# Inverse roots of the norms in a two-model transformer kernel: ScalarE square root and VectorE reciprocal in place of ScalarE logarithm and exponential

## The reference, cut to what matters

```python
def rms_norm(x, g):
    xf = x.astype(jnp.float32)
    y = xf * lax.rsqrt(jnp.mean(xf * xf, axis=-1, keepdims=True) + EPS)
    return (y * g.astype(jnp.float32)).astype(x.dtype)

def layer_norm_2(x, g, b):
    x32 = x.astype(jnp.float32)
    mu = jnp.mean(x32, axis=-1, keepdims=True)
    var = jnp.mean(jnp.square(x32 - mu), axis=-1, keepdims=True)
    y = (x32 - mu) * lax.rsqrt(var + LN_EPS)
    return (y * g.astype(jnp.float32) + b.astype(jnp.float32)).astype(x.dtype)
```

## Time and profile before

| what | value |
|---|---|
| median of 3 runs | 2807.53 us (2806.54 to 2808.13) |
| profiled execution, its own time | 2807.95 us |
| span of the profile | 2806.1 us |
| PE busy | 2563.7 us, 91% |
| DVE busy | 1681.4 us, 60% |
| ACT busy | 1043.4 us, 37% |
| POOL busy | 1098.3 us, 39% |

### The profile page before, as it was taken

One profiled execution on the slowest core, in us unless ns is written; L12 is line 12 of the kernel. 1 busy time (PEld: TensorE's weight loads), 2 busy tenths in 40 slices (PEclk: granted clock), 3 DMA queues, 4 the chain that ended last, 5 costly groups with the idle time before them and its releaser, 6 DMA issues.

```text
span 2806.1 us, 30111 instructions
## 1 busy us (share of the span) xinstructions
PE 2563.7 (91%) x11016; PEld 1998.1 (71%) x11016; DVE 1681.4 (60%) x1987; ACT 1043.4 (37%) x1369; POOL 1098.3 (39%) x375
## 2 busy tenths in 40 slices
PE   4979999996999699999989987999997789799996
PEld 3747888875777478888777865788885446588885
DVE  5986765756444467477439646652665455663565
ACT  4434322333556442223334242632434123542332
POOL 4843444433244144444333353334443034243442
PEclk9989999998999899999999998999998899899998
DMA  4213645523221156464242302224322111233321
GB/s 135 61 38 105 195 157 180 176 85 91 76 67 54 38 150 193 147 192 147 83 120 79 92 29 68 75 75 113 98 79 69 32 60 31 61 95 93 105 82 61
DMA packets 398589, 272.65 MB, mean 97 GB/s; under 512 B 11108, under 2 KB 380772, under 8 KB 398477
## 3 DMA queue, kind: packets, MB, share of 16 engines
q1 hardware_dynamic: 384652, 220.84, 27.7%
q10 hardware_dynamic: 13824, 50.34, 4.9%
HBM read 269.03 MB, written 2.12 MB: 97 GB/s over the span
## 4 chain that ended last, share of the span: by engine, by line
PE 73%; DVE 10%; issue 7%; ACT 4%; POOL 4%; DMA 0%; SPq 0%; DVEq 0%; POOLq 0%; ACTq 0%
PE ps L645 22%; PE ps L647 21%; PE ps L646 21%; POOL weight_lo L1897 3%; DVE ps L1655 2%; PE ps L821 1%; PE ps L887 1%; DVE u_lo L1175 1%; PE ps L806 1%; ACT tmp L2086 1%; ACT u_hi L2087 1%; POOL arena L1910 1%; PE ps L1121 1%; DVE tmp L1170 1%; PE ps L921 1%
## 5 line engine op out<-in xcount | busy, mean ns | idle before, releaser
L1897 POOL TENSOR_TENSOR weight_lo<-weight_raw,weight_hi 128x2048 fp32r<-128x2048 f32 (+2 forms) x224 | 925.9, 4134 | 1502.3 <-ACT weight_hi L2002 1502.3
L645 PE MATMUL ps<-u_hi,weight_hi 128*128 128x512 f32 x2336 | 930.8, 398 | 107.6 <-DVE u_lo L1175 95.9
L646 PE MATMUL ps<-u_lo,weight_hi 128*128 128x512 f32 x2336 | 917.8, 393 | 0.0
L647 PE MATMUL ps<-u_hi,weight_lo 128*128 128x512 f32 x2336 | 917.2, 393 | 0.0
L645 PEld LDWEIGHTS ps<-u_hi,weight_hi 128*128 128x128 f32 x2336 | 444.3, 190 | 226.8 <-DVE u_lo L1175 96.8
L2002 ACT ACTIVATE weight_hi<-weight_raw 128x2048 fp32r<-128x2048 f32 (+2 forms) x224 | 382.4, 1707 | 552.3 <-PE ps L647 533.2
L646 PEld LDWEIGHTS ps<-u_lo,weight_hi 128*128 128x128 f32 x2336 | 444.5, 190 | 95.4 <-issue 4.1
L647 PEld LDWEIGHTS ps<-u_hi,weight_lo 128*128 128x128 f32 x2336 | 443.7, 190 | 94.3
L645 PE MATMUL ps<-act_hi,weight_hi 128*128 128x512 f32 x704 | 274.4, 390 | 2.0 <-DVE act_lo L1175 2.0
L647 PE MATMUL ps<-act_hi,weight_lo 128*128 128x512 f32 x704 | 273.9, 389 | 0.0
L646 PE MATMUL ps<-act_lo,weight_hi 128*128 128x512 f32 x704 | 273.9, 389 | 0.0
(11 more groups left out here) (271 smaller groups left out, 2589.2 us busy)
## 6 DMA issues: line engine op xcount, KB each, us to landing
weight_raw<-in_ffn_w_up SPq DMA_DIRECT2D x132, 512.0 KB, 5.2
arena<-in_ada_w ACTq DMA_DIRECT2D x96, 512.0 KB, 5.9
weight_raw<-in_ffn_w_down SPq DMA_DIRECT2D x64, 704.0 KB, 4.5
weight_raw<-in_ffn_w_gate SPq DMA_DIRECT2D x44, 512.0 KB, 4.0
weight_raw<-in_ev_w_in SPq DMA_DIRECT2D x10, 1024.0 KB, 5.3
weight_raw<-in_conv_w_pw SPq DMA_DIRECT2D x16, 512.0 KB, 6.1
weight_raw<-in_ple_w_gate SPq DMA_DIRECT2D x16, 512.0 KB, 3.7
weight_raw<-in_attn_w_qkv SPq DMA_DIRECT2D x16, 512.0 KB, 4.9
```

What stands on the lines that cost most here:

```text
L645: pe.matmul(bank, w[0], x[0], start=start, stop=False)
L646: pe.matmul(bank, w[0], x[1], start=False, stop=False)
L647: return pe.matmul(bank, w[1], x[0], start=False, stop=stop)
L1897: pool.tensor_tensor(w_lo[r][:, 0:width], raw[r][:, 0:width], w_hi[(k0 + j) % HI_RING][:, 0:width].bitcast(F32), ALU.subtract).then_inc(w_ ...
```

## The change

`inverse_root` issues one ACTIVATE, a square root of scale * sum + eps, which raises `rinv_done`. At each place DVE, behind its wait for `rinv_done`, takes the reciprocal of the 128x512 tile in place and waits for its end (`link`) before it goes on. `ln_table_ahead` loads the set of the square root. The `mark` argument is no longer used. The logarithms and exponentials in `qkv_attention` (L2293, L2301, L2305, L2308) stay as they are.

```diff
@@ rms_apply, ln_apply, up_stage, ple_stage
                 dve.wait_ge(rinv_done, n.next(rinv_done))
+                link(dve.reciprocal(rinv[0], rinv[0]))
...
@@ latent chunks
                     dve.wait_ge(rinv_done, n.next(rinv_done))
+                    link(dve.reciprocal(rinv[0 if i < 3 else 1], rinv[0 if i < 3 else 1]))
...
             def ln_table_ahead():
 
-                sc.preload_act_table_set("natural_log")
+                sc.preload_act_table_set("sqrt_and_others")
...
             def inverse_root(src, scale, eps, to, done=rinv_done, mark=None):
 
-                link(sc.activation(to, src, ACT.Ln, bias=eps, scale=scale))
-                if mark is not None:
-                    sc.sem_inc(mark, 1)
-                sc.activation(to, to, ACT.Exp, scale=-0.5).then_inc(done, 1)
+
+                sc.activation(to, src, ACT.Sqrt, bias=eps, scale=scale).then_inc(done, 1)
```

## The result

The changed kernel takes 2820.15 us (median of 5, 2818.16 to 2822.79) against 2807.63 us (2806.54 to 2808.9): ratio 1.0046, 95% interval 1.0031 to 1.0061. It is slower by 0.46%, more than the 0.2% that a measurement tells from no change. The forecast was 2819 us, slower. The profiled execution took 2820.15 us, so the two profiles differ by 12.2 us.

What follows compares the result with a forecast made beforehand. The prediction took PE's matmuls as the bound, busy 91% of the span. Terms 8.3 + 1.2 + 1.0 + 0.8 gave +11.4 us on 2807.95, so 2819 us, range 2815 to 2823 (0.45); 2811 to 2831 held 8 in 10.

Steps and rivals of the forecast that it cites:

- PE's standstills are what the change moves: PE is busy 91% of the span with untouched matmuls; the change can move only time where PE stands still.
- What is removed, 1.98 us, and no drain behind the load: At place 8, table load, exponential and gaps go, 1.98 us; a further 1.38 us of drain was given no chance.
- R = 3.3 us: Duration of DVE's added reciprocal of 512 columns, priced from 4-column reciprocals by charging every column alike.
- Six places, +1.39 each, 8.3: Layer norms 2, 8, 9, 12, 13 and norm 5: PE waits there, so +1.39 us each counts, +8.3 together.
- Place 4 +1.23 and place 7 +1.03: Side inputs: a later Sigmoid delays POOL's `weight_lo`, for which PE waits; +1.23 and +1.03 us.
- Places 10 and 11, +0.8: Two reciprocals and five products on DVE, two logarithm table loads gone: 2R - 5.85, +0.8 us.
- Places 1, 3 and 6, nothing: Reciprocal hidden under POOL's operation at place 1 and by 1.64 us of slack in the feed-forwards 3 and 6: no cost.
- The sum, 11.4, or 10 R - 21.7 with its zero at 2.17 us: All places added, R being the reciprocal's duration: +11.4 us, 2819 us; the kernel gets faster with R under 2.17 us.
- The chances: For the whole kernel: slower 0.78, within 0.2% 0.10, faster 0.12.
- R of 4.2: Rival: the 512-column reciprocal takes 4.2 us, giving 2828 us, 2824 to 2832; chance 0.27.
- Absorption: Rival: part of the places' delay disappears in a shorter slow stretch of PE; 2812 us, 2808 to 2814; chance 0.10.
- The rival at stream rate: Rival: the reciprocal costs about an ordinary product, 0.71 us, so the kernel gets faster by 12, 2796 us; chance 0.12.

Runs made afterwards that it cites:

- `half`: Changed kernel with each of the 13 reciprocals cut to 256 columns and the square root made a constant 1: 2804.95 us.
- the second trace: Changed kernel, unaltered, run and profiled once more: 2821.86 us, ratio 1.004 against the kernel before.
- `covered`: Changed kernel with a second reciprocal behind the first at places 1, 3 and 6 only: 2828.65 us.
- `early_up`: Changed kernel without the reciprocal at places 3 and 6 (feed-forwards), the other 11 kept whole: 2855.4 us.
- `oneset`: Kernel before with the preloaded table set replaced by one holding both logarithm and exponential, both operations kept: 2828.97 us median, 2801.79 in the profiled run.

## Why the prediction was right, step by step

- *PE's standstills are what the change moves*: right. Eight of the 13 places make up 11.1 of the 12.2 us of difference.
- *What is removed, 1.98 us, and no drain behind the load*: right. In the new table load at L2209 the exponential starts at once:

```profile
2296.17 1.28 ACT L2209 ACT_TABLE_LOAD   x1
...
2297.47 0.37 ACT L2209 ACTIVATE arena<-ps,small 128x128 f32<-128x128 f32 x1
...
2299.14 0.69 ACT L2209 ACTIVATE arena<-ps,small 128x512 f32<-128x512 f32 x1 [0.20 <-DVE small L1562]
```

  2296.17 + 1.28 is 2297.45; the first exponential starts 0.02 us later, and the fourth still waits 0.20 us for DVE. The load cost nothing, with 0.20 us to spare.
- *R = 3.3 us*: 3.35. The reading that charges each column alike held; the other two (0.71 and 4.2) are out. It was the choice on which the answer hung, and it rested on 23 ns in a group of small operations. Between 3.3 and 4.2 the rows hardly told; that the right one was taken was luck in part, and the chances of 0.45 and 0.27 say so.
- *Six places, +1.39 each, 8.3*: measured 1.44 to 1.47, together 8.7; the difference is R's 0.05.
- *Place 4 +1.23 and place 7 +1.03*: 1.33 and 1.05. PE's wait for `weight_lo` was 1.9 us at both; 2.0 and 1.9 were given.
- *Places 10 and 11, +0.8*: +0.7 on DVE, 0.3 at PE's first matmul behind the pooling work. The arithmetic on DVE held, and the pooling work passes a delay on whole: from `half` to the changed kernel that matmul comes 3.19 us later at these places, for two reciprocals longer by 1.60 us each. What no row of before could tell is the gap in the pooling work that is 0.36 us shorter in the changed kernel. The 0.1 at the next load is luck of PE's pace; it was 1.0 in the second trace.
- *Places 1, 3 and 6, nothing*: right, and `covered` shows how much slack was left at place 1 (3.35 us of reciprocal cost 2.5). At place 3 1.0 of 1.64 us of slack was to be used; 0.28 was, since POOL's operation is no longer lengthened by DVE's. That a hidden reciprocal is free was still too narrow: `early_up` shows that without the reciprocal places 3 and 6 cost 34 us. The cover has two edges, and I looked at one of them.
- *The sum, 11.4, or 10 R - 21.7 with its zero at 2.17 us*: the places give 11.2, the slope is 9.5 to 9.6 and the zero 2.03. That the time came within 1.2 us of the forecast owes something to chance: steps of up to 1.6 us outside the places, most of them not the change's, nearly cancel.
- *The chances*: the terms given for slower add to 0.80 (0.45 + 0.27 + 0.03 + 0.05), not 0.78.
- *The rivals.* R of 4.2 fell with the first group of rows. Absorption fell with the ledger (1.44 to 1.47 at each of the six places) and with `half`: 9.5 us for each us. The rival at stream rate was out since R isn't 0.71; had it been, its 2796 us would likely have been wrong for another reason, since VectorE would have started 1.2 us earlier in the up stages, where `oneset` lost 30 us.

## What to carry to other kernels

A small operation that is already in the trace can price a large one: here its excess over its neighbours, charged to every column, came within 2%, though two other readings of the same rows were open until the run. Charge the excess only to where the next engine stands still, and add the places up one by one. An operation that is hidden is not therefore neutral: before making an engine earlier, see which operations of two engines now follow each other closely, since an earlier start can put one behind the other. And where a pair of functions changes tables, look first for a set that holds both or for one operation that does the work of two: here that was worth 20 us, but only with the up stages' order kept.

## What the runs showed of the hardware

- RECIPROCAL on f32 tiles: 177 ns for 4 columns, 1.75 us for 256, 2.75 for 416, 3.35 for 512: 6.25 ns for each column and 0.15 us, while a product of 512 columns takes 0.69 us.
- A DVE operation with two inputs in SBUF (128x1024) that starts 0.2 to 0.4 us behind a POOL operation lasts until 1.08 us after POOL's end (5.30 and 5.48 us in place of 1.28). The other way round, POOL's took 5.50 us in place of 4.60 when DVE's had started 0.27 us ahead. A reciprocal on DVE beside the same POOL operation isn't held.
- One operation (Abs_reciprocal_sqrt) gives the inverse root at the price of a square root, 0.72 us.
- After the same idle time of PE, 2.2 us, the granted clock was 0.88 and 0.78 in one execution of a kernel and 1.00 in two others of it. After a wait of 2.15 us for POOL it was 0.84 and 0.82 in `covered`, and the wait cost twice its length.
